# The filler products of a hybrid decoder step's mixing stage, taken out

## The chip, the cores and the metric

The kernel runs on one core of one Trainium2 chip. The metric is the device time of one execution in microseconds, the median of several; lower is better. TensorE multiplies matrices into PSUM, VectorE (DVE) and ScalarE (ACT) work on its results, GpSimd (POOL) and SyncE (SP) issue most DMAs here. TensorE's clock is granted at one of two levels, 1.2 or 2.4 GHz; the profile shows it as 0.50 and 1.00.

## The reference

One inference step of a two-layer decoder on 512 prompt tokens and 64 sample tokens (8 sequences of 8), width 1024, all in float32:

```python
for l in range(DEPTH):
    mix, st = mixing_block(hp, ...)                       # prompt
    hp = layer_norm(ALPHA * hp + mix, ln1_g[l], ln1_b[l])
    hp = layer_norm(ALPHA * hp + hier_moe(hp, *moe_w), ln2_g[l], ln2_b[l])
    mix, st = mixing_block(hs, ..., past)                 # sample, with a paged cache
    ...
# mixing_block: z = x @ w_in + b_in, then four head groups of 4 heads x 64
#   A  u * (tril(W_s) v + b_s) in chunks of 128
#   B  retention with decay, chunkwise, state r (64 x 64 a head)
#   C  mLSTM, chunkwise, states c, n, m with a running maximum
#   D  softmax attention with forget gates; sample rows also over 2048 cached positions
# out = (normalised, concatenated groups) @ w_out
# hier_moe: top group of 4, then top 2 of its 4 experts
```

## The kernel before, in words

Each engine runs a program of its own, written by hand in the order in which it is to execute; semaphores join them (`pe.wait_ge(sem, n)` holds TensorE, `.then_inc` releases others). `tensor_layer` is TensorE's program for one layer: the input projection (lines 2000, 2038), then the mixing stage, the output projection (2346, 2350), the router and the expert rounds.

The mixing stage takes tokens in blocks of 128, four of the prompt and one of 64 sample rows. The loop from line 2175 on does retention (B), the one from line 2204 on the mLSTM (C), the steps from 2246 on the prompt's attention (D). Between their steps `cache_steps` (2171) puts in pieces of the sample attention over the cache: 72 steps, eight for each of 8 sequences and eight to finish. A step transposes gathered keys (`ps<-tab,kbuf`, 2144), multiplies the keys of the step before with the queries (2107), and by its number turns scores (2117), turns the maxima (2161), spreads the maxima over all partitions by a diagonal (2165) or multiplies with the values (2126 to 2131).

In B and C a block runs: transposes of q and k (`turn_qk`, 1921), ScalarE copies them out, scores (2057), VectorE masks them, products with the values (2073) and the state (2078; for the sample block 32 products, 2082), the state's update (2196, 2235). In the sample block the update is `sample_update`: for each of four heads TensorE waits for VectorE's keys (`km_sb`) and multiplies (2090), with a cache step behind each. C has also a product that lays the gates out as rows (2215) and one for the last maxima (2226). After D, `turn_merged` transposes the merged outputs (2304), line 2318 collects the sample rows, and the output projection begins once `w_out` has landed.

At some of its waits TensorE first does products whose result nobody reads. They multiply the identity with a table of 512 columns into a PSUM bank that is free at that time:

```python
def keep_busy(bank, times):                                  # 1885
    for _ in range(times):
        mm(ps[:, bank, :], idn, T("dec"), start=True, stop=True)   # 1888
```

They stand in front of the wait for VectorE's keys in both `sample_update` (2086, two products), of the diagonal in cache step 4 of each sequence (2163, one, so eight a layer), of the score operands in B's block 1 (2183, one), of the retention state before C (2202, two), of the mLSTM state in C's sample block (2208, one), of C's gates in block 3 (2213, three), of the row maxima in C's sample block (2224, two) and between the last transposes (2322, two). That is 23 products a layer. Each is two matmuls in the trace.

Of the kernel before, what the change touches and what calls it, by code (L numbers as in the profile page):

```python
# [37 lines left out]
NP = NT - 1  # L38
# [200 lines left out]
def decoder(nc, d):  # L239

    ctx = ExitStack()
    with ctx:
# [15 lines left out]
        def T(name, n=P):  # L258
            at, w = TABLE_COLS[name]
            return tab[0:n, at:at + w]  # L260
# [28 lines left out]
        ps = ctx.enter_context(nc.psum_tensor("ps", [P, 8, SLAB], F32))  # L289
# [1589 lines left out]
        def tensor_layer(pe, layer, due):  # L1879
            L, upto = slice(layer, layer + 1), counted(layer)  # L1880
            mm = nc.tensor.matmul
            tr = nc.tensor.transpose
            idn = T("ident")

            def keep_busy(bank, times):

                for _ in range(times):
                    mm(ps[:, bank, :], idn, T("dec"), start=True, stop=True)  # L1888

            def turn_x(t, base, at):  # L1890

# [111 lines left out]
            for i, u in enumerate(UNITS[layer]):  # L2003
# [14 lines left out]
                at, t = u  # L2018
# [11 lines left out]
                for k in range(KD):  # L2030
# [8 lines left out]
                    else:  # L2039
                        for half in range(2):  # L2040
                            m = mm(ps[half * NS:(half + 1) * NS, i % 4, 0:w // 2], xTv[:, k, SEQ:TOK], slab[at][:, k, half * w // 2:(half + 1) * w // 2],
                                   start=(k == 0), stop=(k == KD - 1))
# [40 lines left out]
                m.then_inc(sem, 1)  # L2083

            def sample_update(w, val, place):
                keep_busy(5, 2)
                for h in range(HEADS):
                    pe.wait_ge(km_sb, due(km_sb))
                    for bp in range(BP):
                        m = mm(place(bp, h), km[0:NS, 2 * bp:2 * bp + 2, :].rearrange("p a b -> p (a b)"), val(h), start=True, stop=True)  # L2090
                    m.then_inc(km_used, 1)
                    cache_steps(1)
# [7 lines left out]
            def cache_scores(u):  # L2100

                r, pair, j = u // 2 % 4, u % 2, u // 8
                pe.wait_ge(e_ksb, upto(e_ksb, u + 1))
                if u % 8 == 0 and j >= 1:
                    pe.wait_ge(e_rsb, upto(e_rsb, j))
                for a in range(4):
                    m = mm(ps[a * HQ:(a + 1) * HQ, 1, r * P:(r + 1) * P], qz[:, pair, j, :], kTs[u % 2][:, a * P:(a + 1) * P],  # L2107
                           start=(pair == 0), stop=(pair == 1))
                m.then_inc(e_row, 1)
# [24 lines left out]
            def cache_step(u):  # L2134

                i, g = u // 8, u % 8
                j = i - 1
                if i < DEC_BATCH:
                    if g % 4 == 0:
                        pe.wait_ge(k_in[g // 4], upto(k_in[g // 4], 16 * (i + 1)))  # L2140
                    if u >= 1:
                        pe.wait_ge(e_ksb, upto(e_ksb, u))
                    for a in range(4):
                        m = tr(ps[:, 0, a * P:(a + 1) * P], kv[:, g // 2 * 4 + a, g % 2 * P:(g % 2 + 1) * P], idn)  # L2144
                    m.then_inc(e_kps, 1)
                if u >= 1 and u <= 8 * DEC_BATCH:
                    cache_scores(u - 1)
                if j >= 0 and g == 0:
                    if j > 0:
                        pe.wait_ge(e_xs, upto(e_xs, j))  # L2150
                    c = NEW + j % 2 * HQ
                    for pair in range(PAIRS):
                        m = mm(ps[0:NS, 3, c:c + HQ], kTn[:, pair, :], qz[:, pair, j, :], start=(pair == 0), stop=(pair == 1))
                    m.then_inc(e_psum, 1)
                if j >= 0 and g == 1:
                    turn_scores(j)
                if j >= 0 and g == 2:
                    pe.wait_ge(e_pm, upto(e_pm, j + 1))
                    if j >= 1:
                        pe.wait_ge(e_ym, upto(e_ym, j))  # L2160
                    tr(ps[0:HQ, 3, MT:MT + P], pmax, idn).then_inc(e_mt, 1)
                if j >= 0 and g == 4:
                    keep_busy(2, 1)
                    pe.wait_ge(e_dg, upto(e_dg, j + 1))
                    mm(ps[:, 3, BC:BC + HQ], T("ones", HQ), pdiag[0:HQ], start=True, stop=True).then_inc(e_bc, 1)
                if g == 7 and j >= 0:
                    cache_values(j)
# [3 lines left out]
            def cache_steps(n):  # L2171
                for _ in range(n):
                    cache_step(next(steps))


            for t in tiles:
                n = rows[t]
                if t > 0:
                    pe.wait_ge(b_state, upto(b_state, t))
                turn_qk(t, "b_q", "b_k", 4, b_T)  # L2180
                cache_steps(B_STEPS[0])
                if t == 1:
                    keep_busy(6, 1)
                pe.wait_ge(b_Tsb, upto(b_Tsb, 2 * t + 2))
                scores(t, b_sc)
                if t == NP:
                    sample_queries()
                val = lambda h: zt[0:n, t, COLS["b_v"] + h * HD:COLS["b_v"] + (h + 1) * HD]
                cache_steps(B_STEPS[1])
                pe.wait_ge(b_sw, upto(b_sw, t + 1))  # L2190
                mixed(t, ret, rs, HD, val, b_out)
                pe.wait_ge(b_kd, upto(b_kd, t + 1))
                if t < NP:
                    for pair in range(PAIRS):
                        c = COLS["b_v"] + pair * P
                        m = mm(ps[:, 5, pair * P:(pair + 1) * P], kd[:, pair * P:(pair + 1) * P], zt[:, t, c:c + P], start=True, stop=True)
                    m.then_inc(b_up, 1)
                else:
                    sample_update(HD, val, lambda bp, h: ps[:, 4 + bp // 2, (bp % 2 * HEADS + h) * HD:(bp % 2 * HEADS + h + 1) * HD])
                cache_steps(B_STEPS[2])  # L2200

            keep_busy(2, 2)
            pe.wait_ge(b_state, upto(b_state, NT))
            for t in tiles:
                n = rows[t]
                W = HD + 1
                if t == NP:
                    keep_busy(2, 1)
                if t > 0:
                    pe.wait_ge(c_cd, upto(c_cd, t))  # L2210
                turn_qk(t, "c_q", "c_k", 4, c_T)
                if t == NP - 1:
                    keep_busy(5, 3)
                pe.wait_ge(c_dg, upto(c_dg, t + 1))
                m = mm(ps[0:n, 5, 0:HEADS * n], T("ones", n)[:, 0:n], diag[0:n, :, 0:n], start=True, stop=True)
                m.then_inc(c_row, 1)
                cache_steps(C_STEPS[0])
                pe.wait_ge(c_Tsb, upto(c_Tsb, 2 * t + 2))
                scores(t, c_sc)
                if t == NP:  # L2220
                    sample_queries()
                cache_steps(C_STEPS[1])
                if t == NP:
                    keep_busy(2, 2)
                pe.wait_ge(c_mt, upto(c_mt, t + 1))
                mm(ps[0:n, 5, 0:2 * HEADS], T("last" if t < NP else "last_s", n), mtb[0:n, :], start=True, stop=True).then_inc(c_last, 1)
                cache_steps(C_STEPS[2])
                val = lambda h: vx[0:n, h, :]
                pe.wait_ge(c_sw, upto(c_sw, t + 1))
                pe.wait_ge(c_vx, upto(c_vx, t + 1))  # L2230
                mixed(t, mem, cs, W, val, c_out)
                pe.wait_ge(c_kd, upto(c_kd, t + 1))
                if t < NP:
                    for pair in range(PAIRS):
                        m = mm(ps[:, 5, pair * 2 * W:(pair + 1) * 2 * W], kd[:, pair * P:(pair + 1) * P],
                               vx[:, 2 * pair:2 * pair + 2, :].rearrange("p a b -> p (a b)"), start=True, stop=True)
                    m.then_inc(c_up, 1)
                else:
                    sample_update(W, val, lambda bp, h: ps[:, 4 + bp, h * W:(h + 1) * W])
                    for bp in range(BP):  # L2240
                        m = mm(ps[:, 7, CU + bp * HEADS:CU + (bp + 1) * HEADS], T("last_of", NS)[:, bp * P:(bp + 1) * P], ge[0:NS, HEADS:], start=True, stop=True)
                    m.then_inc(c_up, 1)
                cache_steps(C_STEPS[3] if t < NP else 1)
# [75 lines left out]
            m.then_inc(e_fin, 1)  # L2319

            turn_merged(4)
            keep_busy(2, 2)
            for i in range(NT, 2 * NT):
                turn_merged(i)
            pe.wait_ge(wout_in, upto(wout_in, 32))
# [11 lines left out]
            for at, t in enumerate(OUT_ORDER):  # L2337
                n = rows[t]
                bank = 2 * (at % 2)
# [30 lines left out]
            for t in tiles:  # L2370
                m = mm(ps[:, 1, (t + 1) * EXPERTS:G + EXPERTS].rearrange("p (t e) -> p t e", e=EXPERTS), T("ones"), rep(r_pick[:, t, :], NT - t),
                       start=False, stop=(t == NP))
# [170 lines left out]
```

## Time and profile before

| | us |
|---|---|
| median of 3 runs (1621.38 to 1628.12) | 1621.9 |
| the profiled execution | 1625.71 |
| its span, first to last instruction | 1623.9 |
| TensorE busy (89% of the span) | 1449.6 |
| VectorE busy (45%) | 730.9 |
| ScalarE busy (19%) | 314.7 |
| line 1888, matmuls, busy | 53.7 |
| line 2144, key transposes, busy | 88.3 |

Layer 0's mixing stage reaches from about 221 to 491 us of the span, layer 1's from about 1005 to 1276. A busy TensorE is not one at its peak: matmuls overlap and their ends are modelled. In timeline rows the number in brackets at the end is the engine's idle time before the row, and what ended it; without brackets the engine came straight from the row before.

### The profile page before, as it was taken

What the parts mean: (1) busy time and instruction counts of PE and PEld (TensorE: products, weight loads), DVE (VectorE), ACT (ScalarE), POOL (GpSimd) and SP (SyncE); (2) the same over time, 40 slices, a digit from 0 to 9 for tenths busy, and PEclk for the clock granted to TensorE, in tenths of its full rate; (3) what the DMA queues carried; (4) which work ended last, traced back from release to release, by engine and by line L of the source; (5) the groups of instructions that cost most, each with busy time, mean ns of one, the idle gap of its engine ahead of it and who ended that gap; (6) DMA issues with size and microseconds to landing.
All of it is one profiled execution on the core that took longest, in us unless ns stands there. A gap on an engine that the chain in (4) does not pass through costs nothing.

```text
span 1623.9 us, 20130 instructions
## 1 busy us (share of the span) xinstructions
PE 1449.6 (89%) x7676; PEld 813.9 (50%) x7676; DVE 730.9 (45%) x1525; ACT 314.7 (19%) x651; POOL 129.3 (8%) x118
## 2 busy tenths in 40 slices
PE   8999988889989969999599999888899996999980
PEld 3565556545654535554246554655556444455440
DVE  1294644765583431111527664366557535111116
ACT  1100022332330101111211010233323001121112
POOL 0000200100000041000200011010100001300002
PEclk9999999899779969999799999899977996999995
DMA  9116945456444259999802213553673305799985
GB/s 293 60 46 200 305 130 187 147 160 137 99 148 137 81 185 346 405 413 391 289 20 106 94 43 114 157 195 131 145 156 130 106 0 207 272 405 406 398 326 177
DMA packets 138352, 314.48 MB, mean 194 GB/s; under 512 B 52004, under 2 KB 83748, under 8 KB 117156
## 3 DMA queue, kind: packets, MB, share of 16 engines
q1 hardware_dynamic: 108720, 191.37, 33.3%
q0 software_dynamic: 12672, 86.51, 16.9%
q10 hardware_dynamic: 16884, 35.55, 6.0%
q8 instruction: 51, 0.84, 0.2%
q14 instruction: 25, 0.20, 0.0%
HBM read 266.05 MB, written 47.35 MB: 193 GB/s over the span
## 4 chain that ended last, share of the span: by engine, by line
PE 61%; DVE 17%; issue 14%; DMA 4%; ACT 2%; POOL 1%; ACTq 0%; POOLq 0%; DVEq 0%; SPq 0%
PE ps L2000 10%; PE ps L2038 7%; PE ps L2346 7%; PE ps L2412 4%; DVE ring L1191 4%; DVE z L1191 4%; PE ps L2144 3%; PE ps L2419 2%; PE ps L2449 2%; PE ps L1888 2%; DMA kbuf<-in_cache_k,idx_k 2%; PE ps L2107 2%; PE ps L2126 1%; PE ps L2073 1%; PE ps L2277 1%
## 5 line engine op out<-in xcount | busy, mean ns | idle before, releaser
L1191 DVE TENSOR_TENSOR z<-z,ps 128x512 f32<-128x512 f32 (+1 forms) x102 | 57.6, 586 | 293.3 <-ACT z L889 208.8
L889 ACT ACTIVATE ring<-ps 128x512 f32<-128x512 f32 (+2 forms) x186 | 95.9, 539 | 320.5 <-PE ps L2144 172.3
L2038 PE MATMUL ps<-ring,xT 128*128 128x512 f32 (+1 forms) x384 | 144.7, 535 | 0.8 <-ACT xT L889 0.8
L889 ACT ACTIVATE z<-ps 128x512 f32<-128x512 f32 (+3 forms) x137 | 71.6, 535 | 370.8 <-PE ps L2412 130.8
L2412 PE MATMUL ps<-ring,z 128*128 128x512 f32 x304 | 140.7, 617 | 2.3 <-ACT z L889 1.6
L2000 PE MATMUL ps<-ring,x 128*128 128x512 f32 x320 | 139.1, 593 | 0.0
L2038 PEld LDWEIGHTS ps<-ring,xT 128*128 128x128 f32 x384 | 73.3, 194 | 65.3 <-issue 60.7
L2000 PEld LDWEIGHTS ps<-ring,x 128*128 128x128 f32 x320 | 60.5, 190 | 74.8 <-issue 74.1
L2144 PE MATMUL ps<-tab,kbuf 128*128 128x128 f32 x512 | 88.3, 299 | 7.3 <-ACT ring L889 3.1
L2412 PEld LDWEIGHTS ps<-ring,z 128*128 128x128 f32 x304 | 58.1, 196 | 71.2 <-issue 70.1
L1191 DVE TENSOR_TENSOR z<-ps,vbuf 128x512 f32<-128x512 f32 (+3 forms) x68 | 36.9, 542 | 112.6 <-PE ps L2038 71.3
L889 ACT ACTIVATE xT<-ps 128x512 f32<-128x512 f32 (+3 forms) x88 | 38.7, 474 | 199.8 <-PE ps L1899 194.5
L2144 PEld LDWEIGHTS ps<-tab,kbuf 128*128 128x128 f32 x512 | 63.5, 153 | 19.9 <-issue 8.5
L2419 PE MATMUL ps<-ring,z 128*64 128x256 f32 x608 | 69.8, 382 | 0.1
L1191 DVE TENSOR_TENSOR ring<-ps,ring 128x512 f32<-128x512 f32 (+5 forms) x84 | 38.6, 477 | 67.2 <-PE ps L2268 44.3
L2449 PE MATMUL ps<-ring,z 128*128 128x512 f32 x152 | 68.6, 594 | 0.0
L2000 PE MATMUL ps<-ring,xT 128*128 128x512 f32 x128 | 63.3, 651 | 0.0
L2107 PE MATMUL ps<-ring 128*32 128x128 f32 x1024 | 58.2, 302 | 0.0
L2346 PE MATMUL ps<-kbuf,xT 128*128 128x512 f32 x128 | 57.0, 598 | 0.0
L2346 PE MATMUL ps<-ring,xT 128*128 128x512 f32 x128 | 56.2, 592 | 0.0
L841 POOL DMA_INDIRECT kbuf<-in_cache_k,idx_k x32 | 30.1, 941 | 312.4 <-PE ps L2144 311.2
L1888 PE MATMUL ps<-tab 128*128 128x512 f32 x92 | 53.7, 695 | 0.0
(277 smaller groups left out, 2027.4 us busy)
## 6 DMA issues: line engine op xcount, KB each, us to landing
ring<-in_w SPq DMA_DIRECT2D x114, 1024.0 KB, 9.2
ring<-in_w_in SPq DMA_DIRECT2D x9, 2048.0 KB, 9.4
expert_rows<-zero SPq DMA_DIRECT2D x1, 13056.0 KB, 60.6
expert_rows<-z ACTq DMA_DIRECT2D x19, 512.0 KB, 7.8
z<-expert_rows ACTq DMA_DIRECT2D x17, 512.0 KB, 10.5
z<-expert_rows ACTq DMA_DIRECT2D x19, 256.0 KB, 8.8
expert_rows<-z ACTq DMA_DIRECT2D x38, 128.0 KB, 6.1
ring<-in_w_in SPq DMA_DIRECT2D x4, 1024.0 KB, 8.1
```

The source lines that it names most:

```text
L841: pool.indirect_dma_start(kbuf[:, half * w:(half + 1) * w], None, ck, bass.IndirectOffsetOnAxis(idx_k[:, half, b:b + 1], 0)).then_inc(k_in ...
L889: return nc.scalar.activation(out, in_, fn, **kw)
L1191: return V.tensor_tensor(out, a, b, op)
L1888: mm(ps[:, bank, :], idn, T("dec"), start=True, stop=True)
L2000: m = mm(ps[:, bank, :], turned[:, k, :], part[:, k, :], start=(k == 0), stop=(k == QK - 1))
L2038: m = mm(ps[0:n, i % 4, 0:w], xTv[:, k, t * P:t * P + n], slab[at][:, k, 0:w], start=(k == 0), stop=(k == KD - 1))
L2107: m = mm(ps[a * HQ:(a + 1) * HQ, 1, r * P:(r + 1) * P], qz[:, pair, j, :], kTs[u % 2][:, a * P:(a + 1) * P], start=(pair == 0), stop=(pair ...
L2144: m = tr(ps[:, 0, a * P:(a + 1) * P], kv[:, g // 2 * 4 + a, g % 2 * P:(g % 2 + 1) * P], idn)
L2346: m = mm(ps[0:n, bank + hf, :], xTv[:, k, t * P:t * P + n], w_out[hf][:, k, :], start=(k == 0), stop=(k == KD - 1))
L2412: m = mm(ps[:, 2, :].rearrange("p (w f) -> p w f", w=2), xgT[0][:, q, :], w13[0][:, :, q, :], start=(q == 0), stop=(q == KD - 1))
L2419: m = mm(ps[w * HALF:(w + 1) * HALF, 3, 0:2 * BLOCK], xgT_half[:, q, :], w13[1][:, w, q, :], start=(q == 0), stop=(q == KD - 1))
L2449: m = mm(ps[:, 4 + hf, :], hT[0][:, c, :], w2[0][:, c, hf * SLAB:(hf + 1) * SLAB], start=(c == 0), stop=(c == 1))
```

## The change

All calls of `keep_busy` and the function itself are taken out. Nothing else differs: each wait stands where it stood, and every other instruction of TensorE and of the other engines keeps its order.

```diff
-            def keep_busy(bank, times):
-
-                for _ in range(times):
-                    mm(ps[:, bank, :], idn, T("dec"), start=True, stop=True)
...
             def sample_update(w, val, place):
-                keep_busy(5, 2)
                 for h in range(HEADS):
                     pe.wait_ge(km_sb, due(km_sb))
...
                 if j >= 0 and g == 4:
-                    keep_busy(2, 1)
                     pe.wait_ge(e_dg, upto(e_dg, j + 1))
...
                 cache_steps(B_STEPS[0])
-                if t == 1:
-                    keep_busy(6, 1)
                 pe.wait_ge(b_Tsb, upto(b_Tsb, 2 * t + 2))
...
-            keep_busy(2, 2)
             pe.wait_ge(b_state, upto(b_state, NT))
...
-                if t == NP:
-                    keep_busy(2, 1)
                 if t > 0:
                     pe.wait_ge(c_cd, upto(c_cd, t))
                 turn_qk(t, "c_q", "c_k", 4, c_T)
-                if t == NP - 1:
-                    keep_busy(5, 3)
                 pe.wait_ge(c_dg, upto(c_dg, t + 1))
...
                 cache_steps(C_STEPS[1])
-                if t == NP:
-                    keep_busy(2, 2)
                 pe.wait_ge(c_mt, upto(c_mt, t + 1))
...
             turn_merged(4)
-            keep_busy(2, 2)
             for i in range(NT, 2 * NT):
```

## Rows read from the trace of the kernel before

**Rows 1.** Chain of waits, stretches 200 to 500 and 990 to 1290 us, shares by line
```profile
by line: DVE ring L1191 7.5%; PE ps L2144 7.0%; PE ps L2000 6.8%; PE ps L2126 5.0%; PE ps L1888 4.7%; DMA kbuf<-in_cache_k,idx_k 4.4%; PE ps L2107 4.2%; PE ps L2073 3.6%; PE ps L2277 3.6%; issue 3.4%; PE ps L2266 3.3%; DVE small L1444 2.9%;
...
by line: PE ps L2144 7.6%; DVE ring L1191 6.8%; PE ps L1888 5.2%; DMA kbuf<-in_cache_k,idx_k 5.0%; PE ps L2000 4.9%; PE ps L2107 4.6%; PE ps L2073 3.8%; PE ps L2277 3.7%; issue 3.6%; PE ps L2266 3.2%; PE ps L2126 2.8%; DVE small L1444 2.5%;
```

**Rows 2.** Instructions of line 1888: count, shortest/median/longest in ns, first and last start
```profile
L1888 PE MATMUL ps<-tab x92: 591/592/1222, 229.6 to 1270.1; 128*128 128x512 f32 x92
```

**Rows 3.** Timeline of TensorE around fillers: start us, us, line, op, count
```profile
229.58 1.13 PE L1888 MATMUL ps<-tab 128*128 128x512 f32 x2
...
263.84 1.10 PE L2090 MATMUL ps<-z,xT 64*128 64x64 f32 x8
...
343.43 1.11 PE L2073 MATMUL ps<-ring 128*128 128x65 f32 x8
...
375.34 1.12 PE L1888 MATMUL ps<-tab 128*128 128x512 f32 x2
...
430.33 2.08 PE L1888 MATMUL ps<-tab 128*128 128x512 f32 x2
...
1220.16 1.67 PE L1888 MATMUL ps<-tab 128*128 128x512 f32 x2
```

**Rows 4.** Timeline of ScalarE and VectorE before the waits behind fillers
```profile
228.90 0.66 ACT L889 ACTIVATE ring<-ps 128x256 f32<-128x256 f32 x2 [0.91 <-PE ps L1921]
...
262.75 0.68 DVE L1191 TENSOR_TENSOR xT<-ring,tab 64x512 f32<-64x512 f32 x1
...
341.73 0.69 DVE L1191 TENSOR_TENSOR ring<-ps,ring 128x512 f32<-128x512 f32 x1
...
472.46 0.42 DVE L1191 TENSOR_TENSOR z<-ps,small 128x256 f32<-128x256 f32 x1
473.41 0.19 DVE L1454 COPY small<-ps 128x32 f32<-128x32 f32 x1 [0.53 <-PE ps L2165]
```

**Rows 5.** Stretches: us, busy PE, PEld, DVE, ACT, POOL, granted clock, DMA, GB/s
```profile
279.20:282.60 3.40, 3.40 (x8) 1.71 (x7) 2.87 (x7) 0.16 (x1) 0.00 (x0) 0.50 0.08 19
...
364.60:368.00 3.40, 3.40 (x32) 3.28 (x32) 0.00 (x0) 0.00 (x0) 0.00 (x0) 0.50 0.63 270
...
422.60:443.00 20.40, 20.40 (x85) 13.13 (x86) 9.32 (x23) 6.07 (x16) 0.00 (x0) 0.50 0.12 50
1023.30:1033.60 10.30, 10.30 (x64) 8.34 (x64) 2.82 (x7) 2.56 (x6) 0.94 (x1) 0.50 0.81 292
```

**Rows 6.** Timeline of TensorE at waits, and the same work at both clocks
```profile
278.47 0.27 PE L2161 MATMUL ps<-tab,small 128*32 128x128 f32 x1 [1.86 <-DVE ring L1427]
...
332.02 2.74 PE L1888 MATMUL ps<-tab 128*128 128x512 f32 x6
...
365.44 3.23 PE L2082 MATMUL ps<-xT 128*64 128x65 f32 x32
368.60 1.99 PE L1888 MATMUL ps<-tab 128*128 128x512 f32 x4
371.39 1.10 PE L2090 MATMUL ps<-ring,xT 64*128 64x65 f32 x8 [0.81 <-DVE xT L1191]
...
373.37 1.10 PE L2090 MATMUL ps<-ring,xT 64*128 64x65 f32 x8
...
487.03 2.36 PE L2304 MATMUL ps<-tab,z 64*128 64x64 f32 x20 [1.30 <-DVE z L1191]
...
1096.37 1.97 PE L2073 MATMUL ps<-ring 128*128 128x65 f32 x8
...
1100.35 1.06 PE L2144 MATMUL ps<-tab,kbuf 128*128 128x128 f32 x4
...
1101.91 1.13 PE L1888 MATMUL ps<-tab 128*128 128x512 f32 x2
...
1150.82 2.08 PE L2082 MATMUL ps<-xT 128*64 128x65 f32 x32
1152.83 1.98 PE L1888 MATMUL ps<-tab 128*128 128x512 f32 x4
```

**Rows 7.** Span and mean granted clock of the core
```profile
core 0: 1623.9 us, clock 0.914
```

## The prediction

> **What bounds the kernel now.** I read four views in this order: the chain of waits, the instructions of the filler's line, the timelines around fillers, and the granted clock by stretch. In the chain the reader is to see that the mixing stage has no single bound: TensorE's short steps, VectorE's serial softmax and gate steps, and key gathers take turns, and line 1888, the filler, holds 4.7% and 5.2% of two stretches of 300 us, 14.1 and 15.6 us [rows 1]. So at most 29.7 us of fillers lie on the path. There are 92 filler matmuls, two for each product, 23 products a layer [rows 2]; one product holds TensorE for about 1.06 us, and for 2 us where the clock is granted at 1.2 GHz (median 592 ns, longest 1222).
>
> **What the removal gives back.** A filler is worth its time only if what TensorE waits for behind it was there already. So I go through the places of a layer, read when the awaited operation ended, and count the time from there to the step behind the filler.
> - Retention block 1: the two ScalarE copies end at 228.90 + 0.66 = 229.56 [rows 4], and the filler starts at 229.58 [rows 3]. All of it goes: 1.0 a layer, 2.0.
> - The diagonal products (line 2163, eight a layer): in each, VectorE's diagonal was ready long before. Four a layer lie where TensorE is what others wait for. One follows the last retention transposes; the copies that TensorE waits for next begin together with it, so I take 0.9 of its 1.06. One in C's block 3 comes before a wait on VectorE's masked scores, ready at 341.73 + 0.69 = 342.42 [rows 4]; TensorE comes to them at 343.43 [rows 3]: 0.95. At 375.34 [rows 3] nothing else is waited for: 1.06. The one in block D runs at the low clock, 2.0 in layer 0 and 1.6 in layer 1 [rows 3]. Sum 4.9 and 4.5, 9.4.
> - The last diagonal product: its effect is VectorE's copy at 473.41, which waited 0.53 for TensorE; VectorE was busy until 472.46 + 0.42 = 472.88 [rows 4]. Only 0.5 a layer, 1.0.
> - The first sample update: VectorE's keys are there at 262.75 + 0.68 = 263.43 [rows 4], the step starts at 263.84 [rows 3]: 0.4. With the start of block C and the diagonal product in C's block 2, where a VectorE operation that ends shortly before the filler does the same, I take 1.5 for both layers (0 to 3).
> - Nothing is gained in front of C's block 3, C's sample block, its row maxima, the second sample update and the last transposes: there the release comes after the filler's end, as at 371.39, with 0.81 of idle time left [rows 6]. Two more diagonal products a layer feed a step that waits next for VectorE or for a key gather.
>
> Sum: 2.0 + 9.4 + 1.0 + 1.5 = **13.9 us given back**, out of 29.7 on the chain.
>
> **What the clock takes.** The fillers stand just where TensorE waits. In the trace an idle time of 1.86 us at 278.47 [rows 6] is followed by a stretch granted 0.50, that is 1.2 GHz of 2.4 [rows 5]. It came back behind the dense filler there. Where light work follows it doesn't come back soon: from 1023.3 TensorE is busy for 10.30 of 10.30 us and stays at 0.50, from 422.6 for 20.40 of 20.40 [rows 5]. Without fillers TensorE stands idle for 2.7 us from 332.02 (the filler's own time), 2.8 from 368.60 (1.99 and the 0.81 left at 371.39) and 3.3 up to 487.03 (two products again, 2.0, and 1.30) [rows 6], in both layers, and so do the start of C, C's sample block and its row maxima. These are all at least as long as the one at 278.47. I price the places by rows at both clocks.
> - Second sample update, four heads: at full clock one head takes 373.37 - 371.39 = 1.98 us [rows 6]. At 1.2 GHz the nearest rows are eight value products, 1.97, and the transposes with scores, 1101.91 - 1100.35 = 1.56 [rows 6], together 3.5. These products are light, VectorE hides nothing, and no dense product comes before the cached values behind the fourth head. 1.5 a head, 6.0 a layer, **12.0**.
> - Just before it: the 32 state products take 3.16 us in layer 0, at 0.50 [rows 5, 6], and 2.0 in layer 1. Layer 1 loses this 1.15 too, and the two pairs of transposes and scores ahead lose some 0.6 each (1.56 against 1.98 - 1.10 = 0.88), 1.2 a layer: **3.5**.
> - First sample update: two heads come before the next dense product, 1.5 each: 3.0 a layer, **6.0**.
> - Start of C, C's block 3 and the dense output projection behind the last transposes: one fall each. The lower bound is 1.15 (the 32 products), the upper the 6.0 of the four heads; VectorE's chain covers a part in C and dense work brings the clock back, so I take 2.0, nearer the lower. C's sample block falls in layer 0 already: 1.0. That is 7.0 a layer, **14.0**.
>
> Sum 35.5, with bounds 14 (one stretch at 1.2 GHz, of about 1 us of loss, at each of 14 places, seven a layer) and 50 (block D, which I cost at nothing since a key gather covers it there, falls some 20 us earlier; where the 32 products lose 1.15 of 3.16 us, 36%, that would be 7 a layer).
>
> What it adds up to: 1625.7 (the profiled execution) - 13.9 + 35.5 = 1647.3. That execution lies 3.8 above the median of the three runs, 1621.9, so the median to expect is **1643.5, rounded to 1644**, 1.4% slower.
>
> A rule of the Trainium skill speaks against such a price. "TensorE: Matmul & The Clock Gate", Part 1, says that for modelling the ramp penalty is below 1% of a typical kernel's span. By it the clock could cost no more than 16.2 us, an estimate, and the sum would be 1624. The trace doesn't bear that out: the mean granted clock of the whole run is 0.914 [rows 7], so 17% of the span, some 280 us, ran at half the clock already.
>
> **The rivals.**
> 1. *The clock doesn't move* (other side). If the fillers don't decide which stretches fall, only the given-back time is left: 1621.9 - 13.9 = 1608, faster. For it: the waits of 1.30 at 487.03 and 0.81 at 371.39 [rows 6] stand without a fall. Against it: the 1.86 at 278.47 has one, and the idle times here are 2.7 to 3.3. It decides from the point where fewer than nine new stretches of 1.5 us appear. Chance 0.04.
> 2. *Short falls only.* Each of 14 places brings one short stretch at a loss of 1.5: 21 - 13.9 = +7, 1629. For it: the present falls at 279.2 and 364.6 last 3.4 us each [rows 5]. Against it: these two end behind fillers. Chance 0.20.
> 3. *Long falls in block D too.* 50 - 13.9 = +36, 1658. For it: a fall holds for 20.4 us there [rows 5]. Against it: the one filler there lies beside a gather that is waited for anyway. Chance 0.15.
> 4. *Both about cancel.* Each of the 14 places loses 1 us, the lower bound, since VectorE and ScalarE hide the rest: 14 - 13.9, 1622. For it: VectorE's copies and softmax steps run beside TensorE at most places. Against it: at the four heads TensorE has no idle time to hide anything (1.98 a head, without a wait in the second [rows 6]). Chance 0.05. The 1% of the Trainium skill's page "TensorE: Matmul & The Clock Gate", Part 1, would come out near this, at 1624; 0.914 speaks against it, so it adds 0.01.
>
> The forecast, long falls in the sample updates and short ones elsewhere, has 0.55.
>
> **How the numbers follow.** 0.5%, or 8.1 us, is about what a measurement of this kernel can tell from no change. Slower by more than that are the forecast, rival 3 and about 0.4 of rival 2: 0.78. Rival 4 and the rest of rival 2 are within: 0.18. Rival 1 is faster: 0.04. The range reaches from rival 4 to just past rival 3: 1623 to 1663.
>
> **What would show it.** Right: line 1888 is gone; the step behind the filler in retention block 1 starts about 1 us sooner after its transposes; the four heads of the second sample update take about 3.5 us each at 0.50 in both layers; the first output projection products start at 0.50; the mean clock is below 0.90. Wrong: heads at 2.0 us and full clock, or a mean clock of 0.91, which makes it rival 1 or 2; block D at 0.50 from its start, rival 3.

## The result, and the profile after

| | before | after |
|---|---|---|
| median of 19 runs each, us | 1621.9 (1609.9 to 1635.1) | 1645.7 (1626.9 to 1665.9) |
| ratio, with its 95% interval | | 1.0121 [1.0086, 1.0157] |
| the profiled execution, its span, us | 1623.9 | 1642.0 |
| mean granted clock | 0.914 | 0.889 |
| TensorE busy, us | 1449.6 | 1435.0 |

The changed kernel is slower by 1.2%, some 20 us (14 to 25). The ratio is that of the mean times, without the three runs of the changed kernel and the two of the kernel before that lie more than 1.5% above their kernel's fastest; the two medians alone would give 1.0147. TensorE's busy time fell by 14.6 us only, though fillers with 53.7 us of busy time are gone: the rest takes it longer.

Span and clock of the changed kernel's core, to be held against [rows 7]:

```profile
core 0: 1642.0 us, clock 0.889
```

Stretches of the changed kernel at 1.2 GHz (the others are left out), with the two mixing stages as a whole in the last two rows (us, busy PE, PEld, DVE, ACT, POOL, granted clock, DMA, GB/s):

```profile
240.70:250.90 10.20, 10.20 (x67) 7.76 (x66) 2.37 (x7) 3.05 (x6) 0.94 (x1) 0.50 0.88 326
268.00:274.80 6.80, 6.80 (x60) 4.27 (x52) 1.71 (x2) 3.04 (x4) 0.94 (x1) 0.50 0.24 58
...
367.00:401.10 34.10, 30.05 (x201) 22.05 (x193) 12.91 (x28) 4.74 (x9) 1.88 (x2) 0.50 0.35 129
428.50:438.70 10.20, 6.29 (x37) 4.16 (x37) 1.92 (x6) 2.30 (x6) 0.00 (x0) 0.50 0.85 263
472.80:486.50 13.70, 11.06 (x54) 9.23 (x58) 12.42 (x22) 6.79 (x10) 0.00 (x0) 0.50 0.22 77
...
1155.50:1189.60 34.10, 30.05 (x201) 22.08 (x196) 12.98 (x29) 4.82 (x9) 1.87 (x2) 0.50 0.36 135
221.00:503.00 282.00, 232.65 (x1922) 158.35 (x1922) 165.82 (x389) 86.03 (x199) 20.78 (x22) 0.81 0.52 151
1016.00:1296.00 280.00, 233.96 (x1929) 159.19 (x1929) 163.61 (x387) 85.86 (x199) 20.70 (x22) 0.80 0.52 149
```

The same two stages of the kernel before:

```profile
221.00:491.00 270.00, 238.55 (x1962) 154.94 (x1962) 164.56 (x388) 85.93 (x199) 20.83 (x22) 0.88 0.54 155
1005.00:1276.00 271.00, 237.66 (x1964) 155.80 (x1966) 164.81 (x389) 86.02 (x199) 20.75 (x22) 0.88 0.53 154
```

What to see: the mixing stage went from 270 to 282 us and from 271 to 280, and its clock from 0.88 to 0.81 and 0.80. Two stretches of 34.1 us, one a layer, are new, and both are in the same place: they begin some 12 us ahead of the second sample update and end with the cached values behind it. TensorE works for 30.05 of these 34.10 us, and the clock still doesn't come back. The rest of the time at 0.50 is scattered.

The timeline of TensorE through the first of these stretches, as [rows 6] have it for the kernel before (start us, us, line, op, count, idle time before and what ended it):

```profile
371.21 1.13 PE L2069 MATMUL ps<-ring 64*64 64x65 f32 x8
372.26 3.73 PE L2078 MATMUL ps<-xT 128*64 128x65 f32 x32
378.81 1.94 PE L2085 MATMUL ps<-ring,xT 64*128 64x65 f32 x8 [2.81 <-DVE xT L1191]
...
382.30 1.97 PE L2085 MATMUL ps<-ring,xT 64*128 64x65 f32 x8
...
386.39 1.97 PE L2085 MATMUL ps<-ring,xT 64*128 64x65 f32 x8
...
389.91 1.97 PE L2085 MATMUL ps<-ring,xT 64*128 64x65 f32 x8
...
393.44 1.87 PE L2226 MATMUL ps<-small,tab 64*128 64x4 f32 x8
...
396.71 3.64 PE L2121 MATMUL ps<-vbuf,ring 128*32 128x256 f32 x32
...
432.40 1.12 PE L2139 MATMUL ps<-tab,kbuf 128*128 128x128 f32 x4 [5.56 <-DMA kbuf<-in_cache_k,idx_k]
...
497.34 4.29 PE L2289 MATMUL ps<-tab,z 64*128 64x64 f32 x20 [3.21 <-DVE z L1191]
501.68 1.11 PE L2334 MATMUL ps<-kbuf,xT 128*64 128x512 f32 x1
```

The wait that the filler filled is now 2.81 us of idle time at 378.81, as long as forecast (2.8). The heads behind it start 3.49, 4.09 (the diagonal's own step, line 2159, lies between) and 3.52 us apart, where a head took 1.98 in [rows 6].

A second reading sets each matmul of the changed kernel against the same one before, without the fillers, and follows how much later it starts. The shift grows or shrinks here (layer 0; the change in layer 1 in the last column, where I name it); between these places it falls where a diagonal filler is gone:

| place | shift at its start and end, us | change | layer 1 |
|---|---|---|---|
| retention block 1 | +1.62, +0.59 | -1.0 | |
| block B behind it | +0.6, +4.8 | +4.2 | -4.3 |
| first sample update, behind its first products | +2.37, +4.90 | +2.5 | +2.4 |
| start of C | +4.90, +5.76 | +0.9 | +0.5 |
| C's block 2 (diagonal filler gone in it) | +5.58, +4.79 | -0.8 | +1.1 |
| C's block 3 | +4.78, +5.97 | +1.2 | +1.2 |
| C's sample block, up to the cached values | +5.27, +6.31 | +1.0 | +1.6 |
| just before the second sample update | +6.31, +7.41 | +1.1 | +2.8 |
| its four heads (diagonal filler of 1.06 gone in between) | +7.41, +13.57 | +6.2 | +6.2 |
| cached values behind them | +13.57, +14.79 | +1.2 | +1.9 |
| key gather of block D | +13.72, +18.91 | +5.2 | +4.6 |
| block D behind it (+21.6 on the way; two diagonal fillers, some 4 us, gone) | +18.9, +9.2 | -9.7 | -7.6 |
| last transposes, first output products | +10.3, +11.4 | +1.1 | 0 |

### The profile page after: what moved, and what is told of

It reads as the page before. It is cut to its first block, busy times and chain, and to the rows that moved or that the text cites. A ratio compares the mean times of both kernels' runs of the same rounds, so it can differ in the third digit from the quotient of the medians.

```text
span 1642.0 us, 19950 instructions
## 1 busy us (share of the span) xinstructions
PE 1435.0 (87%) x7584; PEld 820.4 (50%) x7584; DVE 732.0 (45%) x1525; ACT 314.5 (19%) x651; POOL 129.9 (8%) x118
## 4 chain that ended last, share of the span: by engine, by line
PE 58%; DVE 19%; issue 15%; DMA 5%; ACT 2%; POOL 1%; ACTq 0%; POOLq 0%; DVEq 0%
PE ps L1996 10%; PE ps L2330 7%; PE ps L2034 7%; DVE z L1191 4%; DVE ring L1191 4%; PE ps L2396 4%; PE ps L2139 3%; DMA kbuf<-in_cache_k,idx_k 2%; PE ps L2403 2%; PE ps L2433 2%; PE ps L2102 2%; PE ps L2085 2%; PE ps L2069 1%; PE ps L2121 1%; DVE xT L1191 1%
## 5 line engine op out<-in xcount | busy, mean ns | idle before, releaser
L2139 PE MATMUL ps<-tab,kbuf 128*128 128x128 f32 x512 | 95.6, 317 | 17.4 <-DMA kbuf<-in_cache_k,idx_k 12.2
L2139 PEld LDWEIGHTS ps<-tab,kbuf 128*128 128x128 f32 x512 | 68.8, 163 | 34.7 <-issue 13.1
L2102 PE MATMUL ps<-ring 128*32 128x128 f32 x1024 | 62.5, 322 | 0.0
L2403 PEld LDWEIGHTS ps<-ring,z 128*64 128x64 f32 x608 | 45.0, 137 | 19.6 <-issue 1.8
```

The lines of the kernel that those rows point to most:

```text
L2403: m = mm(ps[w * HALF:(w + 1) * HALF, 3, 0:2 * BLOCK], xgT_half[:, q, :], w13[1][:, w, q, :], start=(q == 0), stop=(q == KD - 1))
```

## The experiments

Twelve kernels ran, in groups of four, four, three and one, numbered as they ran; each group has its own runs of the kernel before, and a ratio is to those. The theory was that of the forecast: TensorE's waits let the clock fall, and the light work behind them, the sample updates above all, is then done at half speed.

| run | what it is | ratio to before [95% interval] |
|---|---|---|
| e1 | before, diagonal products out | 0.9937 [0.9900, 0.9975] |
| e2 | before, products at the long waits out | 1.0200 [1.0150, 1.0249] |
| e6 | before, block 1's product out | 0.9980 [0.9952, 1.0008] |
| e5 | before, second sample update's out | 1.0107 [1.0071, 1.0144] |
| e3 | after, second sample update's back in front of its wait | 0.9992 [0.9945, 1.0039] |
| e7 | after, the same behind its wait | 1.0082 [1.0048, 1.0116] |
| e4 | before, every product with a quarter of its weight columns | 0.9984 [0.9954, 1.0014] |
| e11 | after, both sample updates' and block 1's back | 0.9992 [0.9949, 1.0035] |
| e10 | before, diagonal and block 1's out | 0.9928 [0.9886, 0.9970] |
| e8 | e1 with products behind the row-max wait | 1.0032 [0.9998, 1.0066] |
| e9 | e1 with products in front of it | 0.9879 [0.9831, 0.9927] |
| e12 | e9 without block 1's | 0.9924 [0.9892, 0.9955] |

### The change in three parts

The 23 products a layer fall into eight diagonal ones, one in block 1 and 14 at the long waits. The first run takes out the first part.

```diff
                 if j >= 0 and g == 4:
-                    keep_busy(2, 1)
                     pe.wait_ge(e_dg, upto(e_dg, j + 1))
```

> The kernel before, without the filler in front of the diagonal product (line 2163, eight products a layer); the other 15 a layer stay. Theory A (fillers at waits that are over cost their own time, fillers at long waits hold the clock): 10.4 us come back (9.4 and 1.0 of the prediction), a few more falls cost 0 to 5: 5 to 10 us faster than before, about 1613. Rival B (every filler holds the clock alike, so the price goes by the number of products): 16 of 46 products carry 16/46 of the 24 us: 8 us slower.

Measured: 0.9937, 10 us faster (4 to 16), and a mean clock of 0.922 in its profiled execution. The second run takes out the 14 at the long waits and leaves the other nine:

```diff
             def sample_update(w, val, place):
-                keep_busy(5, 2)
...
-            keep_busy(2, 2)
             pe.wait_ge(b_state, upto(b_state, NT))
...
-                if t == NP:
-                    keep_busy(2, 1)
...
-                if t == NP - 1:
-                    keep_busy(5, 3)
...
-                if t == NP:
-                    keep_busy(2, 2)
...
-            keep_busy(2, 2)
             for i in range(NT, 2 * NT):
```

> The other half: the fillers at the long waits are out (both sample updates, before C, C's sample block, C's block 3, its row maxima, the last transposes; 14 products a layer), those at the diagonal and in retention block 1 stay. Theory A: the whole price of the clock without what came back, 35 us less 1.5: slower than before by 25 to 35 us, so slower than the changed kernel too. Rival B: 28 of 46 products, 28/46 of 24 us: 15 us slower, faster than the changed kernel.

Measured: 1.0200, 32 us slower (24 to 40), from six runs. The third part is block 1's:

```diff
-                if t == 1:
-                    keep_busy(6, 1)
                 pe.wait_ge(b_Tsb, upto(b_Tsb, 2 * t + 2))
```

> The kernel before, with only the one product a layer in retention block 1 taken out. Theory A (the term of the sum: it stands behind finished work and its 1.0 us a layer is given back whole, the clock untouched): 2 us faster, ratio 0.999, and no stretch at 0.50 in block B after it that before has not. Rival B (it holds the clock for the blocks behind it: in the changed kernel layer 0 ran at 0.50 from 240.7 for 10.2 us): such a stretch in at least one layer, 4 us lost in it, so 0 to 6 us slower, ratio 1.000 to 1.004.

Measured: 0.9980, 3 us faster (8 faster to 1 slower). The trace has no stretch at 0.50 in block B in either layer (the first are 275.8 and 1057.5), so rival B falls. The three parts multiply to 0.9937 x 1.0200 x 0.9980 = 1.0115, against 1.0121 for the whole change. So the change is two things of opposite sign in one diff: nine products a layer whose removal gains some 13 us, and 14 whose removal costs some 32.

### Where the 32 us sit

Only the two products in front of the second sample update are out, first from the kernel before, then put back alone into the changed kernel.

```diff
             def sample_update(w, val, place):
-                keep_busy(5, 2)
+                if w == HD:
+                    keep_busy(5, 2)
```

> The kernel before, with only the two products in front of the second sample update taken out; all others stay. Theory A (that wait is where nearly all of the price sits): the four heads start 3.5 us apart at 0.50 in both layers instead of 2.0, the cached values behind them lose 1 to 2 us more, and the time is 15 to 25 us above before, ratio 1.009 to 1.015. Rival B (the price is spread over all the waits, and what put the product back in the third run gained had other reasons): the heads are slow, but block D's key gather hides it, and the time is within 6 us of before.

```diff
                 else:
+                    keep_busy(5, 2)
                     sample_update(W, val, lambda bp, h: ps[:, 4 + bp, h * W:(h + 1) * W])
```

> The changed kernel with one thing put back: the two products a layer in front of the second sample update. Theory A: the four heads behind it run at 2.0 us instead of 3.5 to 3.9 in both layers, and the cached values after them at full clock: 14 to 18 us faster than the changed kernel, so 6 to 10 slower than before. Rival B (price spread evenly): 4 of 46 products, 2 us faster than the changed kernel. Rival C (the clock falls ahead of the place, in the row maxima's wait, and two products don't bring it back): heads at 3.5 or more, no gain.

Measured: 1.0107 for the first, 17 us slower (11 to 23); 0.9992 for the second, some 20 us below the changed kernel's 1.0121. The heads of the run without them (layer 0):

```profile
370.45 1.94 PE L2091 MATMUL ps<-ring,xT 64*128 64x65 f32 x8 [2.81 <-DVE xT L1191]
...
373.94 1.97 PE L2091 MATMUL ps<-ring,xT 64*128 64x65 f32 x8
...
377.47 2.08 PE L1888 MATMUL ps<-tab 128*128 128x512 f32 x2
...
380.04 1.97 PE L2091 MATMUL ps<-ring,xT 64*128 64x65 f32 x8
```

And of the run with them alone:

```profile
369.53 1.98 PE L1888 MATMUL ps<-tab 128*128 128x512 f32 x4
372.32 1.10 PE L2089 MATMUL ps<-ring,xT 64*128 64x65 f32 x8 [0.81 <-DVE xT L1191]
...
374.30 1.10 PE L2089 MATMUL ps<-ring,xT 64*128 64x65 f32 x8
...
376.61 1.10 PE L2089 MATMUL ps<-ring,xT 64*128 64x65 f32 x8
```

The distances are 3.49, 6.10 and 3.52 us against 1.98, 2.31 and 1.97 (the last head of each is not shown), and layer 1 has the same to 0.02. So four products in a program of 1600 us are worth 17 to 20 of them. The diagonal filler that still stands between the second and third head of the upper listing runs at 1.2 GHz itself (2.08), and the heads behind it stay slow in both layers.

That isn't always so. The second run, e2, lacks the two products too, and in both of its layers the third and fourth head come at full clock behind the same filler (layer 0):

```profile
368.34 1.07 PE L2089 MATMUL ps<-ring,xT 64*128 64x65 f32 x8 [2.81 <-DVE xT L1191]
...
370.68 1.97 PE L2089 MATMUL ps<-ring,xT 64*128 64x65 f32 x8
...
374.21 2.07 PE L1888 MATMUL ps<-tab 128*128 128x512 f32 x2
...
376.68 1.10 PE L2089 MATMUL ps<-ring,xT 64*128 64x65 f32 x8
```

What all six layers with no product at this place have in common (changed kernel, e2, e5) is that the clock is down at the second head.

What the other 12 of a layer's 14 products are worth is e2 less e5, some 15 us with an uncertainty of some 10, and only if the two products cost as much in e2 as in e5; e2's trace, with two slow heads a layer and not four, speaks against that. The next run looks at ten of these by themselves: it puts back both sample updates' and block 1's, so that against e1 it lacks only the products of block C and of the last transposes.

```diff
             def sample_update(w, val, place):
+                keep_busy(5, 2)
...
+                if t == 1:
+                    keep_busy(6, 1)
                 pe.wait_ge(b_Tsb, upto(b_Tsb, 2 * t + 2))
```

> The changed kernel with only five products a layer put back: two in front of each sample update and one in retention block 1. Against the first run it lacks the ten in front of block C, its block 3, its sample block, its row maxima and the last transposes. Theory A (the forecast's terms for these places, 7.0 a layer): 12 to 14 us above the first run, ratio to before 1.001 to 1.003, and stretches at 0.50 at the start of C, in C's block 3 and at the first output projection products. Rival B (VectorE's chain hides most of it; in the changed kernel these places cost some 1 us each): 2 to 6 us above the first run, ratio 0.995 to 0.998.

Measured: 0.9992, 9 us above e1's 0.9937, with an uncertainty of some 9 us of its own, so it lies between the two theories and settles neither. The two traces say more: e11 is later than e1 by 8.6 us at the first transposes of C and by 9.1 at the four heads in layer 0, and by 15.2 and 15.9 in layer 1. That is 1.2 us in all for block C, where the forecast's terms make 10; nearly all of the 8.6 arose earlier, in steps in which the two kernels are one program. The stretches at 0.50 are there (276.1, 282.9 and 310.2 in e11), but e1, which keeps the fillers of block C, has as many: 64.6 us at 0.50 in block C of both layers, against 64.8 in e11. So in these two traces the products in block C don't hold the clock there. The kernel before, which has the diagonal products too, has 30.7 there, and yet e1 is the faster by 10 us: little of the added time at half clock reached the end.

### Must the idle time itself be filled?

In this run the two products stand behind the wait, so TensorE idles as in the changed kernel and the dense work comes between the idle time and the heads.

```diff
                     pe.wait_ge(km_sb, due(km_sb))
+                    if w != HD and h == 0:
+                        for _ in range(2):
+                            mm(ps[:, 5, :], idn, T("dec"), start=True, stop=True)
                     for bp in range(BP):
```

> The changed kernel, with the two products of the second sample update put back behind its first wait instead of in front of it, so that they fill no idle time. Theory A (what counts is that dense work stands between the idle time and the light heads): the two products run at 0.50 and take 4 us a layer, then the heads come 2.0 us apart at full clock; 7 to 9 us a layer regained less 4, so 6 to 10 us faster than the changed kernel, ratio to before 1.006 to 1.010. Rival B (what counts is that the idle time itself is filled; once the clock has fallen two products do not bring it back): the heads stay at 3.5 us, 4 us a layer are added, and the time is 8 us above the changed kernel, ratio 1.016 to 1.020.

Measured: 1.0082, 6 us below the changed kernel, where theory A put it, though the two intervals overlap. The trace takes neither side whole. In layer 0 the products ran at 1.2 GHz (3.58 us) and the heads came at full clock, 2.01, 2.31 and 1.97 apart:

```profile
377.39 3.58 PE L2086 MATMUL ps<-tab 128*128 128x512 f32 x4 [2.81 <-DVE xT L1191]
380.90 1.13 PE L2088 MATMUL ps<-ring,xT 64*128 64x65 f32 x8
...
382.91 1.10 PE L2088 MATMUL ps<-ring,xT 64*128 64x65 f32 x8
```

In layer 1 they ran as slowly (3.75), and the heads stayed at 3.53, 4.10 and 3.53, in this stretch:

```profile
1149.00:1179.70 30.70, 27.89 (x161) 18.81 (x158) 9.57 (x20) 3.53 (x6) 1.88 (x2) 0.50 0.19 61
```

So dense products behind the idle time can bring the clock back, but don't always, and cost up to 4 us; in front of the wait, in nine kernels (before, e1, e3, e4, e6, e9 to e12), all four heads started at full clock in 18 layers of 18. Only in e8, told below, they lost it. The hold doesn't reach much farther: in four of the 18 (both of e10, layer 1 of e1, layer 0 of e3) the clock fell at the end of the fourth head, with TensorE busy throughout, and the step behind it took 1.87 us as in the changed kernel.

### How heavy must a filler be?

The weights of every product are cut from 128 columns to 32, and the number and place of the products stay.

```diff
-                    mm(ps[:, bank, :], idn, T("dec"), start=True, stop=True)
+                    mm(ps[0:32, bank, :], idn[:, 0:32], T("dec"), start=True, stop=True)
```

> The kernel before with all 46 fillers, but each uses 32 of the identity's 128 columns as weights: TensorE is occupied as long, with a quarter of the multiplying. If the clock is held by TensorE being occupied: as before, within 5 us, mean clock about 0.91. If it goes by how much is multiplied: the falls of the changed kernel, with none of the 13.9 us given back: 25 to 35 us slower than before, mean clock 0.89 or less.

Measured: 0.9984, no change, and 0.931 of mean clock. The filler's line and a head behind it:

```profile
364.49 1.91 PE L1888 MATMUL ps<-tab 128*32 128x512 f32 x4
367.28 1.10 PE L2090 MATMUL ps<-ring,xT 64*128 64x65 f32 x8 [0.89 <-DVE xT L1191]
```

A product that fills a quarter of the columns takes as long (median 592 ns by its line) and keeps the heads at full clock as the whole one does. So "dense", the forecast's word for the fillers, isn't shown to be what counts. What sets them apart from the light heads wasn't tried.

### A version faster than both

Two gains are there to be joined, the diagonal products and block 1's out of the kernel before:

```diff
-                    keep_busy(2, 1)
                     pe.wait_ge(e_dg, upto(e_dg, j + 1))
...
-                if t == 1:
-                    keep_busy(6, 1)
                 pe.wait_ge(b_Tsb, upto(b_Tsb, 2 * t + 2))
```

> The kernel before without the eight diagonal products a layer and without the one in retention block 1, the two places whose removal alone made it faster (ratios 0.994 and 0.998). Theory A (the terms add up): 13 us below before, ratio 0.990 to 0.993, heads of the second sample update 2.0 us apart at full clock in both layers. Rival B (where both are out nothing dense is left in block B, as in the changed kernel, which ran at 0.50 from 240.7): a stretch at 0.50 of 6 us or more in block B in at least one layer, ratio 0.994 to 0.999.

Measured: 0.9928, 12 us faster than before (5 to 18), heads at full clock in both layers, no stretch at 0.50 in block B: theory A.

Then I tried to place fillers better. In front of the row maxima TensorE idles 1.86 us, at 278.47 [rows 6], and a fall follows. The first attempt put a product there:

```diff
                 if j >= 0 and g == 2:
-                    pe.wait_ge(e_pm, upto(e_pm, j + 1))
                     if j >= 1:
                         pe.wait_ge(e_ym, upto(e_ym, j))
+                    if j in (1, 2, 4, 7):
+                        keep_busy(2, 1)
+                    pe.wait_ge(e_pm, upto(e_pm, j + 1))
```

> The kernel before without the eight diagonal products a layer (as in the first run), and with one product put in front of the wait for the cached scores' row maxima at samples 1, 2, 4 and 7, where TensorE stands idle for 1.4 to 1.9 us and the clock falls right behind (at 279.2 and 364.6 in the kernel before). Theory A (an idle time of that length that is filled costs nothing, and the light work behind it keeps full clock): the stretches at 0.50 in block C's blocks 1 and 2 and behind sample 4 go, 6 to 15 us less than the first run, ratio to before 0.984 to 0.990. Rival B (those falls are hidden behind VectorE, as the forecast assumed for most of C): nothing gained over the first run, ratio 0.992 to 0.996.

Measured: 1.0032, outside both. The edit missed its wait. The idle time belongs to the wait for the earlier sample's result, which the edit had put first, so the product stands behind it:

```profile
361.66 1.13 PE L1888 MATMUL ps<-tab 128*128 128x512 f32 x2 [1.79 <-DVE ring L1427]
362.62 0.27 PE L2163 MATMUL ps<-tab,small 128*32 128x128 f32 x1
```

And it did harm farther on. In both layers the first two heads started at full clock, and then, with TensorE busy without a break, the clock fell behind the second's products:

```profile
371.20:388.30 17.10, 17.10 (x109) 11.27 (x108) 6.04 (x10) 2.93 (x5) 0.94 (x1) 0.50 0.35 120
```

The second attempt puts the product at the head of the step:

```diff
                         pe.wait_ge(e_ksb, upto(e_ksb, u))
+                    if g == 2 and j in (1, 2, 4):
+                        keep_busy(0, 1)
```

> As the run before it with products at the row maxima, at samples 1, 2 and 4, but put at the head of that step, in front of its key transposes, so that the idle time of 1.4 to 1.9 us behind them takes them up. In that run they stood behind the wait for the earlier sample's result, and the trace shows the 1.79 us of idle time still ahead of them. Theory A (a filled idle time is free, and the light work behind it keeps full clock): the idle time ahead of the row maxima falls to below 0.9 us, no stretch at 0.50 in block C's block 1 and behind sample 4, 4 to 12 us below the first run (diagonal products out), ratio 0.986 to 0.991. Rival B (the light heads stand so near the edge that other fillers only move the place where the clock falls): the heads of the second sample update lose full clock in at least one layer and the ratio is 0.994 to 1.004.

Measured: 0.9879, in theory A's range, from six runs. The trace agrees only in part. The idle time in front of the row maxima fell from 1.89 to 1.01, not below 0.9:

```profile
357.89 1.12 PE L1888 MATMUL ps<-tab 128*128 128x512 f32 x2
...
360.82 0.27 PE L2163 MATMUL ps<-tab,small 128*32 128x128 f32 x1 [1.01 <-DVE ring L1427]
```

The fall behind sample 4 is gone, but block C of layer 0 has three others (284.5, 305.0, 335.7), together 27.2 us at 0.50, just what e1 has there (273.6 to 362.3); in layer 1 it has 23.9, against e1's 37.4. So I ran it once more, without block 1's product:

```diff
-                if t == 1:
-                    keep_busy(6, 1)
                 pe.wait_ge(b_Tsb, upto(b_Tsb, 2 * t + 2))
```

> The kernel before with the diagonal products and the one of retention block 1 taken out, and one product put at the head of the row-max step of samples 1, 2 and 4: the two changes that gave 0.9928 and 0.9879 in one kernel. Theory A (they add up, the row-max products having taken some 7 us off the kernel without diagonal products, and block 1 some 2): ratio to before 0.984 to 0.989. Rival B (the falls only move elsewhere, and the two gains were the same one, or chance): ratio 0.990 to 0.996, no better than without the row-max products. The heads of the second sample update stay 2.0 us apart at full clock in both layers by either.

Measured: 0.9924, from 12 runs: rival B's range, no better than e10. The row-max products gain nothing that these runs show, and e9's lower figure isn't borne out. What is shown is that the kernel without the diagonal products, with or without block 1's, is faster than both kernels of the case, by 0.6 to 0.7% over before and some 1.9% over after (1.0121 / 0.9928 = 1.019).

## Why the prediction was right, and where its terms were off

The forecast of 1644 and slower by 1.4% met 1645.7 and 1.2% (1.0086 to 1.0157). Of the five signs named for it four came whole: line 1888 is gone; block 1's step starts 1.0 us sooner after its transposes; the heads take 3.5 us at 0.50 in both layers; the clock is 0.889. The fifth came in one layer: the first output projection products ran at 0.50 in layer 0 (1.11 us, at 501.68), in layer 1 only the transposes ahead of them.

- **Given back, 13.9 us.** Right as far as the runs resolve it. The diagonal products with the last one were 9.4 + 1.0 = 10.4; e1 measured 10. Block 1 was 2.0; e6 measured 3 and the timeline 1.0 a layer. No run measured the last term, 1.5, by itself.
- **The long waits, 35.5 taken less 1.5 given back = 34.0.** Right as a sum: e2 measured 32, and the shifts named in the next four points make 33.8 against 35.5. But two of its parts were off by some 6 us each, in opposite directions; that they cancelled is luck.
- **Second sample update, 12.0: too small.** e5 measured 17. A head costs 1.5 us more, as worked out, and four make 6; but the stretch doesn't end with the fourth head. The shift grows by 6.15 + 1.06 (the diagonal filler that went from between the heads) + 1.22 = 8.4 us in layer 0 and 6.16 + 1.06 + 1.85 = 9.1 in layer 1, 17.5. What comes beyond 12 is the step behind the fourth head (line 2226, 1.87 us against 1.05 before) and the cached values (3.64 at 396.71; before 2.84). The step that failed is "no dense product comes before the cached values behind the fourth head": they are the end I took, and they didn't bring the clock back before they were done.
- **Just before it, 3.5.** Measured 1.1 + 2.8 = 3.9. Right, with layer 1 the larger as forecast.
- **First sample update, 6.0.** Measured 2.5 + 2.4 = 4.9.
- **Start of C, C's block 3, its sample block and the output projection, 14.0: too large.** The shift gives 0.9 + 1.2 + 1.0 + 1.1 in layer 0 and 0.5 + 1.2 + 1.6 in layer 1, together 7.5, and e11 against e1 1.2 for block C. The step that failed is "I take 2.0, nearer the lower": the falls came, but in block C e1 has as much time at 0.50 with these fillers as e11 without them, and more of it was hidden than the part that the text gave to VectorE's chain. In the output projection a wait of 1.78 us for the weights (before, at 491.17) took up most.
- **Block D, at nothing.** Wrong in its parts, about right in sum. The key gather landed later (TensorE waited 5.56 us instead of 0.39 in layer 0, 6.63 instead of 2.08 in layer 1), and behind it block D of layer 0 ran at full clock for longer: 23.9 us at 0.50 against the 20.4 and 17.0 of before. The gather took 5.2 and 4.6; block D, its two fillers' some 4 us left out, gave back 6 and 4. The "key gather covers it" of the forecast isn't what made the sum come near nothing.
- **The rivals.** "The clock doesn't move" falls by 0.889 and by e5. "Both about cancel" falls by the interval's lower end, 1.0086. "Short falls only" falls by the two stretches of 34.1 us, though half of the forecast's case against it was misread: of the two falls that "end behind fillers", the one at 364.6 ended at 368.0, during the 32 state products and 0.6 us before the filler at 368.60 [rows 5, 6], so there the clock came back under light work. "Long falls in block D too" falls by 428.5 to 438.7 and 472.8, and its time of 1658 lies above the interval. The Trainium skill's page "TensorE: Matmul & The Clock Gate", Part 1, puts the ramp penalty below 1% of a typical kernel span. It says so of the slow products at a kernel's start, and the forecast stretched it to every fall; no run here times that ramp alone. For the falls of this kernel 1% is too little: the fillers' absence alone cost e2 2.0%, and the clock was at half speed for 22% of the changed kernel's span (twice 1 - 0.889).

## What to carry to other kernels

A filler is judged place by place. In this kernel two questions decided: was what TensorE waits for behind it there already (then it cost its time wherever others waited for TensorE), and is the work behind the wait long, light and with no other engine to hide it (then it paid; the runs show this alone for one place, the second sample update). Here 8 of 23 products a layer cost 10 us and 2 were worth 17, and the time of the whole change told neither. Before a filler is placed, read which wait holds the idle time: behind the wrong one, it is work added.

## What the runs showed that I had not expected

- The clock falls under unbroken light work too. In e8 TensorE was busy for all of 17.10 us from 371.2 while the clock was down, and the two heads ahead had run at full clock. In e1, e3 and e9 to e12 the same heads, with the same short steps between them, kept it into the fourth.
- The same instructions in the same order fall in one execution and not in another. Up to the first sample update e1 and e11 are one program. Layer 0 of e11 ran block B at 0.50 from 238.5:

```profile
238.50:248.70 10.20, 9.86 (x61) 7.92 (x62) 2.82 (x7) 2.56 (x6) 0.94 (x1) 0.50 0.79 286
```

and e1 the same steps, some 3.6 us earlier, at full clock:

```profile
234.90:243.20 8.30, 7.78 (x85) 6.02 (x86) 3.41 (x8) 3.65 (x9) 0.94 (x1) 1.00 0.69 209
```

  So a fall in block B seen in one trace (240.7 after, 1023.3 before [rows 5]) can't be put down to a product taken out or left in. The runs of one kernel differ in how long the clock was down: of the kernel before, in e1's group, the fastest, 1600.2 us, had a mean clock of 0.935 and the slowest, 1633.1, one of 0.913. With such a spread a difference of 0.5% took a dozen runs to see.
- Block D's time at 1.2 GHz in layer 0 was 37.4 us before, 40.8 in e6, 23.9 in the changed kernel and 17.0 in e5, though neither e5 nor e6 touches block D. How much of this follows from work that was shifted ahead of it, and how much is chance, stays open, as does why the key gather took longer: from its issue to the transposes that wait for it 13.3 us before (400.15 to 413.49) and 17.5 after (414.93 to 432.40).
